# Taking out the filler matmuls in front of transposes, scores and router steps

## The chip, the cores and the metric

The kernel runs on one core of a Trainium2 chip. The metric is the device time of one execution in microseconds (us); before the change it was 1500.9 us, the median of three runs (1500.2 to 1502.37).

A core has several engines, each with its own instruction stream: TensorE (PE in the profile; its weight loads are shown apart as PEld), VectorE (DVE), ScalarE (ACT), GpSimd (POOL) and SyncE (SP), which issues the DMAs here. They meet through semaphores: an instruction adds to one, and another engine waits until it has reached a value. TensorE's clock is granted at one of two levels in this trace, 1.00 (2.4 GHz) and 0.50 (1.2 GHz).

## The reference

Two decoder layers on 256 tokens of width 1024, in float32. Each layer adds a token mixer and a channel mixer to the residual x.

```
h    = rms_norm(x, attn_norm_g[layer]);  cols = h @ w_in[layer]
o_a  = mla_mixer(cols A)            # latent attention, 4 heads, causal
o_b  = swa_sink_mixer(cols B)       # window 128, 8 query / 2 key heads, sinks
o_c  = stick_breaking_mixer(cols C) # 4 heads
x    = x + concat(rms_norm each of o_a, o_b, o_c) @ w_out[layer]
h    = rms_norm(x, ffn_norm_g[layer])
x    = x + swiglu(h, dense weights)          # layer 0, hidden width 2816
x    = x + moe_swiglu(h, router, experts)    # layer 1, top 2 of 8, width 3584
```

## The kernel before, in words

Tokens lie in two tiles of 128 (a = 0, 1), the width in eight parts of 128 (k). Weights stream from HBM in units of 2 MB into a ring of seven slots. Each unit is cut into pieces of 1024 columns. Every piece is split into a high part in fp32r (ScalarE, L867, L1016 or L1059) and the rest (VectorE, L1145, L1355 or L1491), and TensorE multiplies in three passes: high x high, high x rest, rest x high (L447 to L449). The activations are split in the same way (hT_hi, hT_lo).

The order on each engine is written out by hand, and TensorE's stream is the one that the change touches. Per layer it is: transposes of the normed input (`transposes(l, "attn_n")`), the input projection in 16 pieces with the latent up-projection among them, transposes for MLA (L500), for window attention (L511, L517) and for stick-breaking (L525), the stick-breaking scores (L538, L540), the scores of MLA and of window attention (L545, L546), the cumulative sums of stick-breaking (L565 to L569), the transposes of probabilities (L575) and the products with the values (L580 to L583), the transposes of the mixed heads (`transposes(l, "mix_n")`), the output projection, and the transposes of the second norm (`transposes(l, "ffn_n")`). Layer 0 goes on with the dense stage. Layer 1 goes on with `experts_prepare`: router logits (L682), then ranks in each expert by five small matmuls (L687 to L691). `experts` then gathers each expert's tokens by matmuls with a selection matrix (L708, L710) and runs over the eight experts.

`transposes` issues 16 transposes (L440) of xn. ScalarE and VectorE copy and split the results out of PSUM (L855, L1135), and the first product waits for the first two parts. The inputs come from a norm: ScalarE squares (L831), a chain of small steps on both engines gives the scale, and both engines write the scaled rows (ScalarE L836 or, for the mixed heads, L994; VectorE L1117 or L1331).

`stay_warm(bank, times)` (L426 to L429) issues matmuls of the identity with 512 columns of constants into a PSUM bank, and nothing reads the result. It is called in nine places in the text. Each float32 matmul of this shape leaves two records in the trace.

Of the kernel before, what the change touches and what calls it, by code (L numbers as in the profile page):

```python
# [176 lines left out]
class Counts:  # L177
# [6 lines left out]
    def at(self, key, it=None, back=0):  # L184
        if self.known is None:
            return 1 if it is None else it + 1
        name, loop, start, m = self.known[key]
        if loop is None:
            return m
        k = self.known["per", loop, name]  # L190
        if it is None:
            return start + (NE - 1) * k + m
        assert start + m - back * k > 0
        return it * k + (start + m - back * k)
# [10 lines left out]
def trunk_program(nc, known, x, cst, smalls, w_in, w_uq, w_ukv, w_out, dense_g, dense_u, dense_d, moe_g, moe_u,  # L205
# [3 lines left out]
    with ExitStack() as ctx:  # L209
        def sb(name, shape, dt=F32):  # L210
            return ctx.enter_context(nc.sbuf_tensor(name, shape, dt))
# [6 lines left out]
        consts = sb("consts", [P, N_CONST])  # L218
# [17 lines left out]
        ps = ctx.enter_context(nc.psum_tensor("ps", [P, 8, 512], F32))  # L236
# [62 lines left out]
        def C(name):  # L299
            a, w = CONST[name]  # L300
            return consts[:, a:a + w]

        def G(name, l=None):
            a, w = SMALL[name] if l is None else SMALL[name, l]
            return small[:, a:a + w]

        ident = C("ident")
# [115 lines left out]
        def _(pe):  # L423
            more = []

            def stay_warm(bank, times):  # L426

                for _ in range(times):
                    pe.matmul(ps[:, bank, :], ident, consts[:, 0:512], start=True, stop=True)  # L429

            def transposes(l, what):

                b0 = 4 if what == "ffn_n" else 0
                if what != "attn_n" or l:
                    stay_warm(0, {"mix_n": 4, "ffn_n": 4, "attn_n": 4}[what])
                for a in range(TT):
                    pe.wait_ge(act_done if a else dve_done, at((what, l, a)))
                for k in range(KD):
                    for a in range(TT):
                        ins = pe.transpose(ps[:, b0 + k // 2, (k % 2) * T + a * P:(k % 2) * T + (a + 1) * P],  # L440
                                           xn[:, a, k * P:(k + 1) * P], ident)
                    if k % 2 == 1:
                        ins.then_inc(pe_done, pe_p.step((what + "_T", l, k // 2)))
# [6 lines left out]

            def layer_mixers(l):
                transposes(l, "attn_n")

                def up_projection():
# [49 lines left out]
                for a in range(TT):  # L504
                    pe.wait_ge(*cols_in_sbuf(l, 2, a))
                pe.wait_ge(const_loaded, 16)
                stay_warm(4, 2)
                pe.wait_ge(dve_done, at(("swa_n", l)))
                for i in range(4):
                    for a in range(TT):  # L510
# [19 lines left out]
                pe.wait_ge(act_done, at(("stickT", l, 0)))  # L530
                pe.wait_ge(dve_done, at(("stickT", l, 1)))
                pe.wait_ge(act_done, at(("mlaT", l, 1)))
                stay_warm(1, 1)
                pe.wait_ge(dve_done, at(("stickT", l, 1)))
                for h in range(HC):
                    o, j = HD * (h % 2), h // 2
# [2 lines left out]
                              start=True, stop=False, skip_group_check=True)  # L539
                    ins = pe.matmul(ps[:, 4 + h, T:SEG], stick_kT[o:o + HD, j, P:T], stick_qT[o:o + HD, j, P:T],  # L540
                                    start=False, stop=False, skip_group_check=True)
# [43 lines left out]
                    ins.then_inc(pe_done, pe_p.step(key))  # L585

                pe.wait_ge(dve_done, at(("sB_read", l, 0)))
                stay_warm(0, 2)
                for h in range(HA):
                    pe.wait_ge(act_done, at(("pA", l, h)))  # L590
                    pe.wait_ge(dve_done, at(("w_read", l, h)))
# [11 lines left out]
                for h in range(HB):  # L603
                    bank = (6, 7, 0, 1, 3, 6, 7, 0)[h]
# [16 lines left out]

                pe.wait_ge(dve_done, at(("oB_read", l, 1)))
                transposes(l, "mix_n")
                for q in range(N_OUT):
                    (_, n), r = L_PIECES[l][q]
# [3 lines left out]
                    for a in range(TT):  # L629
                        for k in (2 * r, 2 * r + 1):  # L630
# [3 lines left out]
                                               k == KD - 1)  # L634
                    ins.then_inc(pe_done, pe_p.step(("piece", l, q)))
                transposes(l, "ffn_n")

            def dense(l):
# [35 lines left out]
            def experts_prepare():  # L674
                l = DEPTH - 1
                pe.wait_ge(small_loaded, 16)

                for i, k in enumerate((0, 1, 4, 5, 2, 3, 6, 7)):
                    if k % 2 == 0:
                        pe.wait_ge(act_done if k < 4 else dve_done, at(("ffn_n_done", l, k // 2)))  # L680
                    for a in range(TT):
                        ins = pe.matmul(ps[:, a, 0:NE], hT[:, k, a * P:(a + 1) * P],  # L682
                                        G("router")[:, k * NE:(k + 1) * NE], start=i == 0, stop=i == KD - 1)
                ins.then_inc(pe_done, pe_p.step("logits"))
                stay_warm(3, 3)
                pe.wait_ge(dve_done, at("selected"))
                pe.matmul(ps[:, 2, 0:NE], C("rank_tri"), sel[:, 0, :], start=True, stop=True)  # L687
                pe.matmul(ps[:, 2, NE:2 * NE], C("ones"), sel[:, 0, :], start=True, stop=False)
                pe.matmul(ps[:, 2, NE:2 * NE], C("rank_tri"), sel[:, 1, :], start=False, stop=True)
                pe.matmul(ps[:, 2, 2 * NE:3 * NE], C("ones"), sel[:, 0, :], start=True, stop=False)  # L690
                ins = pe.matmul(ps[:, 2, 2 * NE:3 * NE], C("ones"), sel[:, 1, :], start=False, stop=True)  # L691
                ins.then_inc(pe_done, pe_p.step("ranks"))

            def experts(group):
                g = group

                def gather(key, it=None):

                    pe.wait_ge(dve_done, at((g, key, "pick"), it))
                    for n in range(2):  # L700
                        if it is not None:

                            pe.wait_ge(dve_done, at((g, "hidT_lo", NCH - 2 - n), it))
                        for k in range(4):
                            for a in range(TT):

                                dims = slice((4 * n + k) * P, (4 * n + k + 1) * P)
                                pe.matmul(ps[:, 6 + n, k * P:(k + 1) * P], xn_hi[:, a, dims], pick[:, a, :],  # L708
                                          start=a == 0, stop=False, skip_group_check=True)
                                ins = pe.matmul(ps[:, 6 + n, k * P:(k + 1) * P], xn_lo[:, a, dims], pick[:, a, :],  # L710
                                                start=False, stop=a == TT - 1, skip_group_check=True)
                        ins.then_inc(pe_done, pe_p.step((g, key, "gathered", n)))
# [7 lines left out]
                                        start=True, stop=True)  # L720
                        ins.then_inc(pe_done, pe_p.step((g, "scatter" + key, q)))

                if g == 0:
                    stay_warm(6, 3)
                gather("first")
                if g == 0:
                    more.append(pe.value_load(over_i[0:1, 0:1], min_val=0, max_val=1))
# [70 lines left out]

            pe.wait_ge(ident_loaded, 16)
            layer_mixers(0)  # L800
            dense(0)
            pe.wait_ge(dve_done, at(("ffn_add", 0, 1)))
            layer_mixers(1)
            experts_prepare()
            experts(0)
            with pe.If(more[0] > 0):
                experts(1)
# [794 lines left out]
```

## Time and profile before

| | |
|---|---|
| median of three runs | 1500.9 us (1500.2 to 1502.37) |
| span of the profiled execution | 1498.5 us |
| TensorE busy | 1458.0 us (97%), 7282 matmul records |
| weight loads | 1209.2 us (81%) |
| VectorE busy | 1210.2 us (81%) |
| ScalarE busy | 1046.6 us (70%) |
| mean granted clock of TensorE | 0.992 |
| HBM | 415.23 MB read, 278 GB/s |

The span runs from the first to the last instruction of the program in one profiled execution; the timed runs are other executions. Busy shares are averages over the whole span. The layers and the work ahead of the experts make up its first 484 us, and the eight experts the rest.

In the rows further down, a row in order of time gives the start and the length in us, engine, line, operation, what it writes and reads, the shape and the number of records merged into it; in brackets the idle time of the engine ahead of it and who ended that. The length of a merged row reaches from its first start to its last end, and records can overlap.

### The profile page before, as it was taken

Reading aid. Unit: us, or ns where it says so; the run is one execution under the profiler, and the core shown is the slowest. Engines: PE = TensorE matmul, PEld = TensorE weight load, DVE = VectorE, ACT = ScalarE, POOL = GpSimd, SP = SyncE. Lnnn points to the kernel's source line nnn. Section 1 sums busy time; section 2 is a strip of 40 time slices with the busy share of each in tenths; the row PEclk is TensorE's granted clock in tenths of the full one; section 3 lists DMA queues with packets and bytes.
Section 4 is the critical chain, followed back from the end, with each engine's and each line's share of the span. In section 5 each row is a group of like instructions: output and inputs, shape, how many; then the busy total and the mean of one; then the engine's idle time right before and its main releaser. Section 6 shows DMA issues by size and latency. Waiting matters only on the chain.

```text
span 1498.5 us, 21039 instructions
## 1 busy us (share of the span) xinstructions
PE 1458.0 (97%) x7282; PEld 1209.2 (81%) x7282; DVE 1210.2 (81%) x1501; ACT 1046.6 (70%) x1452; POOL 0.2 (0%) x4
## 2 busy tenths in 40 slices
PE   7999999999998999999999999999999999999997
PEld 6777999978775788888888878888888887888885
DVE  5666555546765899899899999989989999998995
ACT  5675444435764788788788778878878877887884
POOL 0000000000000000000000000000000000000000
PEclk9999999999998999999999999999999999999999
DMA  9904444454111899899989989989999998998960
GB/s 365 347 1 169 169 169 141 164 219 169 57 58 56 301 372 380 305 373 365 349 330 376 368 311 374 376 306 370 367 347 333 372 370 313 372 372 314 374 225 30
DMA packets 175806, 416.90 MB, mean 278 GB/s; under 512 B 3344, under 2 KB 8080, under 8 KB 175632
## 3 DMA queue, kind: packets, MB, share of 16 engines
q1 hardware_dynamic: 175760, 416.29, 76.1%
q8 instruction: 28, 0.46, 0.1%
q14 instruction: 18, 0.15, 0.0%
HBM read 415.23 MB, written 1.05 MB: 278 GB/s over the span
## 4 chain that ended last, share of the span: by engine, by line
PE 92%; DVE 4%; ACT 3%; issue 1%; DMA 0%; DVEq 0%; SPq 0%; ACTq 0%
PE ps L447 27%; PE ps L448 27%; PE ps L449 27%; PE ps L719 2%; PE ps L742 2%; PE ps L710 1%; PE ps L708 1%; PE ps L429 1%; DVE scratch L1247 1%; PE ps L575 1%; ACT scratch L908 1%; PE ps L580 0%; PE ps L583 0%; PE ps L581 0%; ACT xn L831 0%
## 5 line engine op out<-in xcount | busy, mean ns | idle before, releaser
L1059 ACT ACTIVATE e_hi<-ring 128x1024 fp32r<-128x1024 f32 x672 | 712.2, 1061 | 200.4 <-PE ps L449 200.4
L1491 DVE TENSOR_TENSOR e_lo<-ring,e_hi 128x1024 fp32r<-128x1024 f32 x672 | 793.2, 1219 | 63.9 <-ACT e_hi L1059 47.4
L447 PE MATMUL ps<-e_hi,xgT_hi 128*128 128x512 f32 x896 | 357.2, 399 | 3.5 <-DVE e_lo L1491 3.5
L449 PE MATMUL ps<-e_hi,xgT_lo 128*128 128x512 f32 x896 | 349.9, 391 | 0.0
L448 PE MATMUL ps<-e_lo,xgT_hi 128*128 128x512 f32 x896 | 349.8, 390 | 0.0
L447 PEld LDWEIGHTS ps<-e_hi,xgT_hi 128*128 128x128 f32 x896 | 168.9, 188 | 38.9 <-DVE e_lo L1491 3.7
L448 PEld LDWEIGHTS ps<-e_lo,xgT_hi 128*128 128x128 f32 x896 | 168.9, 188 | 35.4 <-issue 1.9
L449 PEld LDWEIGHTS ps<-e_hi,xgT_lo 128*128 128x128 f32 x896 | 168.6, 188 | 35.6
L1355 DVE TENSOR_TENSOR d_lo<-ring,d_hi 128x1024 fp32r<-128x1024 f32 x82 | 100.2, 1224 | 95.0 <-ACT d_hi L1016 94.7
L447 PE MATMUL ps<-e_hi,hidT_hi 128*128 128x512 f32 x448 | 175.7, 392 | 0.0
L449 PE MATMUL ps<-e_hi,hidT_lo 128*128 128x512 f32 x448 | 174.5, 390 | 0.0
L448 PE MATMUL ps<-e_lo,hidT_hi 128*128 128x512 f32 x448 | 174.4, 389 | 0.0
L1016 ACT ACTIVATE d_hi<-ring 128x1024 fp32r<-128x1024 f32 x82 | 87.0, 1061 | 112.1 <-PE ps L449 112.1
L447 PE MATMUL ps<-hT_hi,d_hi 128*128 128x256 f32 x352 | 99.7, 283 | 1.0 <-DVE hT_lo L1135 1.0
L449 PE MATMUL ps<-hT_hi,d_lo 128*128 128x256 f32 x352 | 99.6, 283 | 0.0
L448 PE MATMUL ps<-hT_lo,d_hi 128*128 128x256 f32 x352 | 99.6, 283 | 0.0
L449 PEld LDWEIGHTS ps<-e_hi,hidT_lo 128*128 128x128 f32 x448 | 84.1, 188 | 17.8
L448 PEld LDWEIGHTS ps<-e_lo,hidT_hi 128*128 128x128 f32 x448 | 84.2, 188 | 17.0
L447 PEld LDWEIGHTS ps<-e_hi,hidT_hi 128*128 128x128 f32 x448 | 84.1, 188 | 16.9
L447 PEld LDWEIGHTS ps<-hT_hi,d_hi 128*128 128x128 f32 x352 | 67.6, 192 | 1.4 <-DVE hT_lo L1135 1.2
L448 PEld LDWEIGHTS ps<-hT_lo,d_hi 128*128 128x128 f32 x352 | 67.6, 192 | 0.2
L449 PEld LDWEIGHTS ps<-hT_hi,d_lo 128*128 128x128 f32 x352 | 67.6, 192 | 0.0
(233 smaller groups left out, 1648.9 us busy)
## 6 DMA issues: line engine op xcount, KB each, us to landing
ring<-moe_g SPq DMA_DIRECT2D x56, 2048.0 KB, 9.0
ring<-moe_u SPq DMA_DIRECT2D x56, 2048.0 KB, 9.4
ring<-moe_d SPq DMA_DIRECT2D x56, 2048.0 KB, 8.5
ring<-w_in SPq DMA_DIRECT2D x6, 2048.0 KB, 10.8
ring<-dense_g SPq DMA_DIRECT2D x5, 2048.0 KB, 8.0
ring<-dense_u SPq DMA_DIRECT2D x5, 2048.0 KB, 8.1
ring<-dense_d SPq DMA_DIRECT2D x5, 2048.0 KB, 8.8
ring<-w_out SPq DMA_DIRECT2D x4, 2048.0 KB, 14.3
```

The costliest lines, as they stand in the source:

```text
L429: pe.matmul(ps[:, bank, :], ident, consts[:, 0:512], start=True, stop=True)
L447: pe.matmul(out, hi_l, hi_r, start=start, stop=False, skip_group_check=True)
L448: pe.matmul(out, hi_l, lo_r, start=False, stop=False, skip_group_check=True)
L449: return pe.matmul(out, lo_l, hi_r, start=False, stop=stop, skip_group_check=True)
L575: ins = pe.transpose(ps[:, bank, j * P:(j + 1) * P], S[:, slot, j * P:(j + 1) * P], ident)
L708: pe.matmul(ps[:, 6 + n, k * P:(k + 1) * P], xn_hi[:, a, dims], pick[:, a, :], start=a == 0, stop=False, skip_group_check=True)
L719: ins = pe.matmul(ps[:, bank, :], pick_gT[:, a, :], ysb[:, n * CH:(n + 1) * CH], start=True, stop=True)
L742: ins = pe.transpose(ps[:, bank, j * P:(j + 1) * P], hid[:, c % 2, j * P:(j + 1) * P], ident)
L1016: nc.scalar.activation(d_hi[:, q % SPLIT, :], slot_of(no)[:, r * PIECE:(r + 1) * PIECE], ACT.Copy).then_inc(act_done, act_p.step(("lead", ...
L1059: nc.scalar.activation(e_hi[:, q % SPLIT, :], slot_of(no)[:, r * PIECE:(r + 1) * PIECE], ACT.Copy).then_inc(act_done, act_p.step((g, "lead ...
L1355: nc.vector.tensor_tensor(d_lo[:, q % SPLIT, :], slot_of(UNIT_NO[kind, l, c])[:, r * PIECE:(r + 1) * PIECE], d_hi[:, q % SPLIT, :].bitcast ...
L1491: nc.vector.tensor_tensor(e_lo[:, q % SPLIT, :], slot_of(no)[:, r * PIECE:(r + 1) * PIECE], e_hi[:, q % SPLIT, :].bitcast(F32), ALU.subtra ...
```

## The change

All nine calls of `stay_warm` and the helper itself are taken out. The calls stood: at the head of `transposes` (four matmuls each for mix_n and ffn_n of both layers, and for attn_n of layer 1; none for attn_n of layer 0); in front of the window-attention transposes (two); in front of the stick-breaking scores (one); in front of the transposes of MLA probabilities (two); behind the router logits (three); and in front of the first gather (three). That makes 36 matmuls in one execution. Every wait stays where it was, and no other instruction changes.

```
-            def stay_warm(bank, times):
-                for _ in range(times):
-                    pe.matmul(ps[:, bank, :], ident, consts[:, 0:512], start=True, stop=True)
...
                 b0 = 4 if what == "ffn_n" else 0
-                if what != "attn_n" or l:
-                    stay_warm(0, {"mix_n": 4, "ffn_n": 4, "attn_n": 4}[what])
                 for a in range(TT):
                     pe.wait_ge(act_done if a else dve_done, at((what, l, a)))
...
                 pe.wait_ge(const_loaded, 16)
-                stay_warm(4, 2)
                 pe.wait_ge(dve_done, at(("swa_n", l)))
...
                 pe.wait_ge(act_done, at(("mlaT", l, 1)))
-                stay_warm(1, 1)
                 pe.wait_ge(dve_done, at(("stickT", l, 1)))
...
                 pe.wait_ge(dve_done, at(("sB_read", l, 0)))
-                stay_warm(0, 2)
                 for h in range(HA):
                     pe.wait_ge(act_done, at(("pA", l, h)))
...
                 ins.then_inc(pe_done, pe_p.step("logits"))
-                stay_warm(3, 3)
                 pe.wait_ge(dve_done, at("selected"))
...
-                if g == 0:
-                    stay_warm(6, 3)
                 gather("first")
```

## Rows read from the trace of the kernel before

**Rows 1.** The page's chain of work that ended last, by engine.

```profile
PE 92%; DVE 4%; ACT 3%; issue 1%; DMA 0%; DVEq 0%; SPq 0%; ACTq 0%
```

**Rows 2.** Instructions of line 429: duration ns min/median/max, first and last start, shape.

```profile
L429 PE MATMUL ps<-consts x72: 590/592/1222, 65.0 to 475.4; 128*128 128x512 f32 x72
```

**Rows 3.** TensorE in order of time, window-attention transposes and stick-breaking scores, layer 0.

```profile
65.03 1.88 PE L429 MATMUL ps<-consts 128*128 128x512 f32 x4
66.75 1.04 PE L511 MATMUL ps<-consts,scratch 128*128 128x128 f32 x8
...
69.71 1.10 PE L429 MATMUL ps<-consts 128*128 128x512 f32 x2 [0.83 <-ACT stick_qT L932]
70.73 0.71 PE L538 MATMUL ps<-stick_qT,stick_kT 64*128 64x256 f32 x4
```

**Rows 4.** VectorE in order of time, the same stretch.

```profile
65.81 0.28 DVE L1235 TENSOR_TENSOR cols<-cols,stat 128x128 f32<-128x128 f32 x1
...
68.92 0.69 DVE L1242 COPY stick_kT<-ps 128x512 f32<-128x512 f32 x1
```

**Rows 5.** TensorE in order of time, transposes of the mixed heads, layer 0.

```profile
102.75 5.34 PE L429 MATMUL ps<-consts 128*128 128x512 f32 x8 [0.85 <-DVE xn L1300]
107.93 1.91 PE L440 MATMUL ps<-consts,xn 128*128 128x128 f32 x16
110.37 0.50 PE L447 MATMUL ps<-d_hi,hT_hi 128*128 128x512 f32 x1 [0.53 <-DVE hT_lo L1135]
```

**Rows 6.** ScalarE and VectorE in order of time, the same stretch.

```profile
105.70 1.52 ACT L994 ACTIVATE xn<-xn,stat 128x256 f32<-128x256 f32 x3 [0.70 <-DVE stat L1109]
...
108.27 1.23 DVE L1355 TENSOR_TENSOR d_lo<-ring,d_hi 128x1024 fp32r<-128x1024 f32 x1 [1.56 <-ACT d_hi L1016]
```

**Rows 7.** TensorE in order of time, transposes of the second norm, layer 0.

```profile
132.27 3.59 PE L429 MATMUL ps<-consts 128*128 128x512 f32 x8
138.25 1.94 PE L440 MATMUL ps<-consts,xn 128*128 128x128 f32 x16 [2.38 <-ACT xn L836]
141.20 0.36 PE L447 MATMUL ps<-hT_hi,d_hi 128*128 128x256 f32 x1 [1.01 <-DVE hT_lo L1135]
```

**Rows 8.** ScalarE and TensorE in order of time, start of layer 1.

```profile
333.21 1.15 ACT L836 ACTIVATE xn<-xres,stat 128x1024 f32<-128x1024 f32 x1 [0.70 <-DVE stat L1109]
...
335.90 1.91 PE L440 MATMUL ps<-consts,xn 128*128 128x128 f32 x16
338.34 0.46 PE L447 MATMUL ps<-in_hi,in_hT_hi 128*128 128x416 f32 x1 [0.53 <-DVE in_hT_lo L1135]
...
338.64 0.35 PE L448 MATMUL ps<-in_lo,in_hT_hi 128*128 128x416 f32 x1
```

**Rows 9.** TensorE in order of time, transposes of MLA probabilities, layer 0.

```profile
81.59 1.88 PE L429 MATMUL ps<-consts 128*128 128x512 f32 x4
83.79 1.91 PE L575 MATMUL ps<-consts,scratch 128*128 128x128 f32 x12 [0.32 <-DVE stick L1289]
```

**Rows 10.** TensorE in order of time, the kernel's start, and the router.

```profile
10.57 3.57 PE L440 MATMUL ps<-consts,xn 128*128 128x128 f32 x16 [10.57 <-ACT xn L836]
...
14.38 0.35 PE L448 MATMUL ps<-in_lo,in_hT_hi 128*128 128x416 f32 x1
...
462.51 1.94 PE L440 MATMUL ps<-consts,xn 128*128 128x128 f32 x16 [2.38 <-ACT xn L836]
464.29 3.64 PE L682 MATMUL ps<-small,hT 128*128 128x8 f32 x32
```

**Rows 11.** Stretches: length, TensorE busy (records), granted clock, DMA share, GB/s.

```profile
467.91:471.31 3.40, 3.40 (x6) 0.50 0.00 0
477.07:480.90 3.83, 3.79 (x32) 1.00 0.01 2
...
484.38:488.38 4.00, 4.00 (x9) 0.50 0.00 0
```

**Rows 12.** VectorE in order of time, ahead of the read of the ranks.

```profile
472.77 2.36 DVE L1435 TENSOR_TENSOR xn_lo<-xn,xn_hi 128x1024 fp32r<-128x1024 f32 x2
```

More of the change, by code:

```diff
@@ L424, in _ @@
             more = []
-            def stay_warm(bank, times):
-                for _ in range(times):
-                    pe.matmul(ps[:, bank, :], ident, consts[:, 0:512], start=True, stop=True)
             def transposes(l, what):
                 b0 = 4 if what == "ffn_n" else 0
-                if what != "attn_n" or l:
-                    stay_warm(0, {"mix_n": 4, "ffn_n": 4, "attn_n": 4}[what])
                 for a in range(TT):
@@ L506, in layer_mixers @@
                 pe.wait_ge(const_loaded, 16)
-                stay_warm(4, 2)
                 pe.wait_ge(dve_done, at(("swa_n", l)))
@@ L532, in layer_mixers @@
                 pe.wait_ge(act_done, at(("mlaT", l, 1)))
-                stay_warm(1, 1)
                 pe.wait_ge(dve_done, at(("stickT", l, 1)))
@@ L587, in layer_mixers @@
                 pe.wait_ge(dve_done, at(("sB_read", l, 0)))
-                stay_warm(0, 2)
                 for h in range(HA):
@@ L684, in experts_prepare @@
                 ins.then_inc(pe_done, pe_p.step("logits"))
-                stay_warm(3, 3)
                 pe.wait_ge(dve_done, at("selected"))
@@ L721, in scatter @@
                         ins.then_inc(pe_done, pe_p.step((g, "scatter" + key, q)))
-                if g == 0:
-                    stay_warm(6, 3)
                 gather("first")
```

## The prediction

> **What bounds the kernel now.** I read the chain of work that ended last first. TensorE holds 92% of it [rows 1], and nearly all of that is the matrix products of the two dense stages and of the eight experts, which the change does not touch. So only those stretches count in which a removed matmul stands on the chain, or in which its absence changes the clock that the next work gets. The second view is the list of one line's instructions: the helper's line 429 has 72 records on TensorE, 592 ns median [rows 2]. A call leaves two records, so 36 filler matmuls run. Four of them took 3.59 us in one place, 0.9 us each, and 5.34 us, partly at the low clock, in another [rows 5, 7]. The third view is the order of time around each call, to see what the next real instruction was waiting for. The fourth is the granted clock by stretch. It shows two levels, 1.00 (2.4 GHz) and 0.50 (1.2 GHz).
>
> **Where a filler itself is in the way (the gains).**
>
> (a) Before the window-attention transposes. The filler runs at 65.03 and the transposes (L511) start at 66.75 [rows 3], but their input is there when VectorE's L1235 ends at 65.81 + 0.28 = 66.09 [rows 4]. From the end of L1242 at 68.92 + 0.69 = 69.61 to TensorE's next start at 69.71 [rows 3, 4] a hand-over takes 0.10 us. So 66.75 - 66.19 = 0.56 us goes. The next in line, VectorE's L1239, is free by then.
>
> (b) Before the stick-breaking scores. All waits are met when the filler starts at 69.71, and the scores start at 70.73 [rows 3]. The whole 1.02 us is in series, and the chain goes on through these scores.
>
> Both come once in each layer, with the same durations in the second: 2 x (0.56 + 1.02) = 3.2 us.
>
> (c) Before the second layer's first transposes. The last input is ScalarE's L836, 333.21 + 1.15 = 334.36, but the transposes start at 335.90, when eight filler records are through [rows 8]. They can start near 334.5, 1.4 us sooner. At the low clock the first four of them take about 0.85 us instead of 0.45, so 1.0 us reaches the ScalarE and VectorE copies behind them and the first product at 338.34.
>
> Gains together: 3.2 + 1.0 = 4.2 us. They are nearly certain, since each is a stretch in which the real work had been ready. Ends: 3.6 and 4.6.
>
> **Where a filler is hidden.** In front of the mixer-output transposes the fillers end late (the transposes start at 107.93 [rows 5], ScalarE's L994 had been done at 105.70 + 1.52 = 107.22 [rows 6]). But the first product, at 110.37, waits for VectorE: L1355 from 108.27 to 109.50 and then two parts of the split [rows 6]. Starting TensorE 0.6 us sooner brings nothing there. In front of both ffn_n transposes the engine was idle for another 2.38 us after the filler [rows 7]. In front of the attention probabilities' transposes the filler begins at 81.59 and L575 waits until 83.79 for VectorE [rows 9]. The five rank matmuls, each of 8 columns, are read by VectorE only after L1435, at 472.77 + 2.36 = 475.13 [rows 12], which leaves room for them at either clock. In front of the gather, TensorE waits for VectorE's pick until 477.07. Taking all these away gives nothing directly; what it does is leave the engine without work.
>
> **What the clock does (the costs).** The clock was at 0.50 from 467.91 to 471.31, after 3.6 us of router matmuls with 8 columns each [rows 10, 11]; it fell again after the gather and stayed low through the first 4.00 us of the expert products, until 488.38 [rows 11]. At the kernel's start, where TensorE had done nothing, 16 transposes took 3.57 us against 1.91 to 1.94 elsewhere, and a 416-column product right behind them, at 14.38, took 0.35 us, the same as one at 338.64 deep in layer 1 [rows 5, 7, 8, 10]. So a burst after a long idle stretch runs at half rate for about 3.5 us, and 4.0 us is the longest that a row shows. That is the price list.
>
> (d) Four places: mix_n in both layers, ffn_n in the first, attn_n in the second. Without filler TensorE has nothing for 5.4 to 6.0 us ahead of its transposes (102.75 - 0.85 = 101.9 to 107.3, and 132.27 to 138.25 [rows 5, 6, 7]; the start of layer 1 waits for the same chain of a norm), so I take it that they begin at 1.2 GHz. They then take 3.57 us, but in pairs, and each pair is followed by ScalarE and VectorE work of about the same length. The product streams start 2.4 (107.93 to 110.37) to 2.95 us (138.25 to 141.20) after the transposes do [rows 5, 7], or 3.1 with the earlier start at mix_n. So 0.4 to 0.6 us of the stream is still at half rate, 0.2 to 0.3 us each: 0.9 us for the four. Ends: 0 (the clock back sooner) and 2.0 (4.0 us low).
>
> (e) ffn_n of the second layer and the router: TensorE is the chain here, 16 transposes in 1.94 us and then 32 router records in 3.64 [rows 10]. The transposes at half rate add 1.65 us. The router's records are as dense as the transposes' and should double too if the clock is low; by rows, thin router work began at 464.29 and lost the clock only at its end, so I add only 0.15: 1.8 us. Ends: 0.3 and 3.5.
>
> (f) The gather: 32 matmuls in 3.83 us at clock 1.00 [rows 11], with a filler ahead of it. Now the engine has only 8-column work from 464.29 [rows 10] and, while VectorE works from 475.13 on [rows 12], none before 477.07. It starts low. With 3.5 us at half rate the price is 1.7; if its 128-column matmuls don't bring the clock back, 3.8. No row shows a gather at a low clock; what it is nearest to is a clock that fell right after it, so I take 2.5, above the middle of 1.0 and 3.8.
>
> (g) The 2.2 us between 81.59 and 83.79 [rows 9] become empty, and the chain gives all of 83.79 to 101.9 to TensorE. A gap of 2.38 us kept its clock at 138.2 [rows 7]; a gap of 0.85 us behind the 64-column products with the values lost it, as the eight filler records of 5.34 us tell [rows 5]. If the clock falls here, about 3.4 us run at half: 1.7 us a layer. I take one layer of the two: 1.7. Ends: 0 and 3.4.
>
> Expert products 484.38 to 488.38: low before and after, no change.
>
> **Sum.** 0.9 + 1.8 + 2.5 + 1.7 - 4.2 = +2.7 us. On the profiled execution's own 1498.5 us span that is 1501.2; the timed runs' median lies 2.4 us higher, at 1500.9, so 1503.6.
>
> One page speaks against this sum. The Trainium skill, "TensorE: Matmul & The Clock Gate", Part 4: PE-mode transpose, says that transposes don't count as activity for the clock. The trace disagrees as far as it goes: the start's 16 transposes were the only work before products that ran at the full rate [rows 10].
>
> **Rivals.**
>
> *The clock mostly holds.* (g) costs nothing and the gather only 1.7: 1503.6 - 1.7 - 0.8 = 1501.1. For it: 2.38 us of idle time were survived [rows 7]. Against: there a dense product stream stood ahead. Chance 0.27.
>
> *Thin work stays slow* (the one that ends slower). Place: the 18 us from 83.79, and the gather. Price: (g) in both layers, +1.7, and the gather at half rate throughout, +1.3: 1506.6. It decides when the gap at 81.59 loses the clock in both layers, and it is past the bound from the moment that the second of these falls happens. For it: the clock did fall behind 64-column products. Chance 0.17.
>
> *Transposes don't bring the clock back.* Then the product stream behind each of the four places of (d) itself runs 3.4 us at half, 1.7 us each in place of 0.23, and the router is slow whole, +3.6: 1503.6 + 5.9 + 3.6 = 1513. This is what the page's rule named above would make of it; the start of the trace speaks against it. Chance 0.05.
>
> *The waits cover the low clock.* The clock comes back early (ends of d, e and g) and the gather pays 1.0: 1500.9 + 0 + 0.3 + 1.0 + 0 - 4.2 = 1498.0. Against: (e) and (f) are on the chain with nothing beside them. Chance 0.09. That the fillers are not really gone is excluded: the diff leaves no call.
>
> **How the numbers follow.** 0.2% is 3.0 us here, about what the measurement can tell from no change, so slower begins at 1503.9 and faster ends at 1497.9. The forecast's case has 0.42, from 1502.3 to 1505, of which 0.19 lies beyond 1503.9. Slower: 0.19 + 0.17 + 0.05 = 0.41. Faster: 0.09 at most. Same: 0.50. The range leaves out the 1513 case, most of the 1498 case and the outer parts of the others: 1499.8 to 1507.8. Both kernels vary from execution to execution with where the clock falls, which the three runs' 2.2 us of spread allow.
>
> **What would show it.** Right: first window-attention transposes about 0.5 us after TensorE's last transposes of MLA, no record between L932 and L538, 16 transposes of 3 to 3.6 us at mix_n and ffn_n with a granted clock of 0.50, transposes and router together near 7.3 us, gather of 5.5 to 7.5 us, first product of mix_n at the same distance from ScalarE's L994. Wrong: 16 transposes of 1.9 us in these places, a gather of 3.8 us (then it is faster), or a clock of 0.50 through the attention values or deep in a product stream (then it is slower than the range's middle).

## The result, and the profile after

The change makes the kernel slower: 1514.03 us median of five runs (1503.79 to 1517.23) against 1500.9 us (1500.2 to 1505.69), a ratio of 1.0074 with a 95% interval of 1.0041 to 1.0108. A repetition on another occasion gave 1.0131 (1.0079 to 1.0182). The prediction was 1503.6, with a range of 1499.8 to 1507.8. It was wrong.

The single runs say more than the median. Here are all nine of the changed kernel, with the mean granted clock of each:

```
us     1503.79  1513.45 1513.47 1513.69 1514.03 1517.10 1517.23  1525.87 1527.17
clock    0.979    0.974   0.974   0.974   0.974   0.972   0.972    0.967   0.965
```

They stand in three groups some 10 us apart, and the time rises as the mean clock falls. The first trace of the changed kernel is of the one run in the lowest group. It is 3.4 us longer than the traced run of before (spans 1501.9 and 1498.5), near the forecast sum of 2.7, and that this one run falls so close to 1503.6 is the luck of the draw. So that trace alone can't tell why most runs are slow; a second one, below, can.

TensorE in order of time in the first trace, window-attention transposes and stick-breaking scores; these answer to [rows 3]:

```profile
66.53 1.06 PE L503 MATMUL ps<-consts,scratch 128*128 128x128 f32 x8 [1.04 <-DVE cols L1222]
...
69.56 0.71 PE L529 MATMUL ps<-stick_qT,stick_kT 64*128 64x256 f32 x4 [0.87 <-DVE stick_kT L1229]
```

And VectorE in the same stretch, answering to [rows 4]:

```profile
66.10 0.28 DVE L1222 TENSOR_TENSOR cols<-cols,stat 128x128 f32<-128x128 f32 x1
...
68.73 0.69 DVE L1229 COPY stick_kT<-ps 128x512 f32<-128x512 f32 x1
```

Both now start 0.14 to 0.15 us after their input ends (66.38 and 69.42). The fillers that stood in between are really gone, and so is their time. (The calls taken out stand in six places of the text, as the edit shows, and not in nine; the count of 36 matmuls is right.)

TensorE in order of time at the transposes of the mixed heads (L433, then the products L440), of the second norm in layer 0, and at the start of layer 1. These answer to [rows 5, 7, 8]:

```profile
106.17 3.32 PE L433 MATMUL ps<-consts,xn 128*128 128x128 f32 x16 [5.47 <-ACT xn L981]
109.24 0.48 PE L440 MATMUL ps<-d_hi,hT_hi 128*128 128x512 f32 x1
...
137.10 3.65 PE L433 MATMUL ps<-consts,xn 128*128 128x128 f32 x16 [5.82 <-ACT xn L823]
140.40 0.56 PE L440 MATMUL ps<-hT_hi,d_hi 128*128 128x256 f32 x1
140.75 0.41 PE L441 MATMUL ps<-hT_lo,d_hi 128*128 128x256 f32 x1
...
334.91 3.30 PE L433 MATMUL ps<-consts,xn 128*128 128x128 f32 x16 [6.41 <-ACT xn L823]
337.96 0.43 PE L440 MATMUL ps<-in_hi,in_hT_hi 128*128 128x416 f32 x1
...
429.73 3.65 PE L433 MATMUL ps<-consts,xn 128*128 128x128 f32 x16 [5.47 <-ACT xn L981]
```

The last row is the same place as the first, in layer 1. All the transposes run at half rate, as forecast. At 140.75 a 256-column product still does, 0.41 us a record where the full clock gives 0.28.

Stretches of the same trace: length, TensorE busy (records), granted clock, DMA share, GB/s. They answer to [rows 11]:

```profile
82.60:102.18 19.58, 18.10 (x148) 1.00 0.01 2
102.20:109.01 6.81, 2.85 (x14) 0.50 0.00 1
136.33:143.14 6.81, 6.04 (x29) 0.50 0.41 138
330.89:337.70 6.81, 2.79 (x13) 0.50 0.01 1
406.50:426.45 19.95, 17.77 (x147) 1.00 0.01 2
426.47:433.27 6.80, 3.54 (x17) 0.50 0.00 0
...
467.43:491.30 23.87, 13.51 (x54) 0.50 0.00 0
476.80:484.40 7.60, 7.08 (x32) 0.50 0.00 1
```

The first and fifth rows are the probability transposes, scores and values of the two layers, at the full clock in this execution. From the router's end to the first expert products the clock is low for 23.87 us, and the gather takes 7.08 us of TensorE instead of 3.79.

And the router, answering to [rows 10]:

```profile
461.01 3.39 PE L433 MATMUL ps<-consts,xn 128*128 128x128 f32 x16 [5.82 <-ACT xn L823]
464.24 3.94 PE L672 MATMUL ps<-small,hT 128*128 128x8 f32 x32
```

### The profile page after: what moved, and what is told of

Same layout as the page of the kernel before. It is cut to its first block, busy times and chain, and to the rows that moved or that the text cites. A ratio compares the mean times of both kernels' runs of the same rounds, so it can differ in the third digit from the quotient of the medians.

```text
span 1501.9 us, 20899 instructions
## 1 busy us (share of the span) xinstructions
PE 1432.2 (95%) x7210; PEld 1207.3 (80%) x7210; DVE 1210.4 (81%) x1501; ACT 1046.9 (70%) x1452; POOL 0.2 (0%) x4
## 4 chain that ended last, share of the span: by engine, by line
PE 92%; DVE 4%; ACT 2%; issue 1%; DMA 1%; SPq 0%; DVEq 0%; ACTq 0%
PE ps L440 27%; PE ps L441 27%; PE ps L442 27%; PE ps L708 2%; PE ps L729 2%; PE ps L699 1%; PE ps L697 1%; PE ps L433 1%; DVE scratch L1234 1%; PE ps L566 1%; DMA ring<-w_in 1%; ACT scratch L895 1%; PE ps L571 0%; PE ps L574 0%; PE ps L572 0%
## 5 line engine op out<-in xcount | busy, mean ns | idle before, releaser
L440 PE MATMUL ps<-e_hi,xgT_hi 128*128 128x512 f32 x896 | 357.4, 399 | 3.5 <-DVE e_lo L1478 3.5
L440 PEld LDWEIGHTS ps<-e_hi,xgT_hi 128*128 128x128 f32 x896 | 168.8, 188 | 38.8 <-DVE e_lo L1478 3.7
L440 PE MATMUL ps<-e_hi,hidT_hi 128*128 128x512 f32 x448 | 175.8, 392 | 0.0
L440 PE MATMUL ps<-hT_hi,d_hi 128*128 128x256 f32 x352 | 100.4, 285 | 0.0
L440 PEld LDWEIGHTS ps<-e_hi,hidT_hi 128*128 128x128 f32 x448 | 84.2, 188 | 16.9
L440 PEld LDWEIGHTS ps<-hT_hi,d_hi 128*128 128x128 f32 x352 | 68.3, 194 | 0.2
```

The lines of the kernel that those rows point to most:

```text
L440: pe.matmul(out, hi_l, hi_r, start=start, stop=False, skip_group_check=True)
```

## The experiments

Means below are over all runs of a kernel, set against the mean of the runs of before in the same batch. The ratio with its interval is a separate estimate from the same runs; it can differ from the quotient of the means by some 0.1% (most in the next experiment: 1.0131, where the means give 1.0114).

**The changed kernel again.**

> The changed kernel unchanged, for a second trace. In its first profiled execution (1501.9 us span, mean granted clock 0.979) the clock kept its full level through the attention values of both layers; the other four runs had spans of 1511.8 to 1515.1 us at a mean clock of 0.974 and 0.972. Theory T1 (the empty gap ahead of the probability transposes loses the clock and the thin products with the values don't get it back): if this execution is a long one, a stretch between about 82 and 102 us, or its twin 324 us later, stands at 0.50 for 10 us or more. Theory T2 (the extra time lies at the router, the gather and the first expert products): those two stretches stand at 1.00 and more of the low clock than before lies between 460 and 500 us. Median expected 1514, with single runs from 1503 to 1518.

Measured: 1519.67 us median of four (1513.45 to 1527.17), ratio 1.0131 (1.0079 to 1.0182). The traced execution had a span of 1511.4 us, of the middle group. Stretches of this trace, the same columns:

```profile
81.00:101.95 20.95, 18.11 (x148) 1.00 0.01 2
405.75:426.21 20.46, 20.46 (x88) 0.50 0.00 1
...
477.43:501.31 23.88, 13.51 (x53) 0.50 0.00 0
```

This is what the first trace could not show. Layer 0 went through its probability transposes, scores and values at 1.00. Layer 1, with the same instructions, went at 0.50 for 20.46 us in which TensorE was busy all the time. At half the rate that is 10.2 us more, the distance between the groups. T1 stands. T2, as the cause of the long runs, does not: the low stretch from the router's end to the first expert products is 23.88 us here and was 23.87 in the short run's trace, and transposes and router together took 7.26 us (from 470.19 to 477.45) against 7.17.

**Only the fillers in the probability gap put back.**

```
+                stay_warm(0, 2)            # ahead of the probability transposes
                 for h in range(HA):
```

> The changed kernel with only the two filler matmuls ahead of the probability transposes put back, in each layer. T1: the long executions vanish, all runs between 1502 and 1506 us, mean clock 0.979 or above. T2: as the changed kernel, most runs at 1513 to 1517.

Measured: 1505.87 median of ten (1503.44 to 1509.65), ratio 1.0024 (1.0010 to 1.0037). No run at 1513 or above. Four runs lie above the expected 1506, at mean clocks of 0.978 and 0.979. These four matmuls (two in each layer) of the 36 are worth 10 us: the mean is 1506.2 against 1516.2 for the nine runs of the changed kernel. Against the mean of before, 1502.8, the other 32 taken out cost 3.4 us (1.5 to 5.6 by the interval), where the prediction's sum without its term (g) has 1.0.

**Only these taken out.**

```
                 pe.wait_ge(dve_done, at(("sB_read", l, 0)))
-                stay_warm(0, 2)
```

> The kernel before with only these two filler matmuls per layer taken out. T1: most runs 8 to 13 us longer than before, so 1509 to 1514, at a mean clock about 0.985; a few at 1501. T2: 1500 to 1502.5, as before.

Measured: 1510.49 median of ten, ratio 1.0052 (1.0018 to 1.0085); mean 1511.0 against 1502.8. The runs again fall into groups:

```
1500.88 1501.16 | 1509.58 1510.07 1510.41 1510.57 1510.61 1511.78 | 1521.54 1523.03
```

Two runs stand where before stands, six some 10 us above, two some 20 us above. With 10.2 us for a layer that reads as none, one and both; a trace shows it for the middle group alone. Stretches of the traced run (1510.07):

```profile
84.00:104.50 20.50, 18.71 (x150) 1.00 0.01 2
408.90:429.36 20.46, 20.46 (x88) 0.50 0.01 2
```

One trace holds both outcomes behind the same idle gap. In order of time, the gap in layer 0, where the clock stayed up:

```profile
82.52 0.39 PE L569 MATMUL ps<-stick,consts 128*128 128x128 f32 x2
84.94 1.91 PE L575 MATMUL ps<-consts,scratch 128*128 128x128 f32 x12 [2.04 <-DVE stick L1288]
```

and in layer 1, where it fell at 408.9, with what followed:

```profile
405.80 0.39 PE L569 MATMUL ps<-stick,consts 128*128 128x128 f32 x2
408.23 2.45 PE L575 MATMUL ps<-consts,scratch 128*128 128x128 f32 x12 [2.04 <-DVE stick L1288]
410.61 0.79 PE L545 MATMUL ps<-swa_kT,swa_qT 64*128 64x128 f32 x2
...
416.51 0.64 PE L581 MATMUL ps<-mla_v,hT 128*128 128x64 f32 x2
...
426.32 2.77 PE L575 MATMUL ps<-consts,scratch 128*128 128x128 f32 x12
...
429.74 0.39 PE L580 MATMUL ps<-cols,hT 128*128 128x64 f32 x2
```

The gap is 2.04 us in both, so its length alone doesn't decide. The clock then stayed low through 12 transposes, the eight 64-row score matmuls of four heads and 24 products of 64 columns (0.64 us for two records against 0.39), and came back only behind the next 12 transposes.

That the empty gap is what lets the clock fall rests on all traces together. Four traces have the gap empty (two of the changed kernel, this one and the next), and in three of the eight passages the clock fell at it, each time in layer 1. In the nine other traces, of before and of the further experiments, the filler stands in the gap, and in none of the 18 passages did a low stretch begin between it and the end of the products with the values.

**A late filler.** Does a fallen clock stay low for a fixed 20 us, or until denser work comes?

```
-                stay_warm(0, 2)            # the probability gap
...
                 for h in range(HA):
                     pe.wait_ge(*probs_in_sbuf(l, "A", h))
+                    if h == 0:
+                        stay_warm(4, 2)
                     values(probsT[:, h, :], ...)
```

> As the kernel with the two probability fillers taken out, but with two 512-column matmuls per layer put behind the first wait of the products with the values, where TensorE is on the chain. In two traces the clock fell at the empty gap and stayed at 0.50 for 20.5 us both times. Theory T1a (the 64-column products can't raise it, dense work can): the low stretch ends within some 7 us behind the late filler, long runs shrink from 1510 and 1521 to 1504 to 1512; runs without a fall pay 1.7 us per layer and stand at 1504. T1b (a fallen clock stays low for a fixed 20 us whatever is run): the low stretch is again 20.5 us, the runs stay at 1510 and more, and the filler adds 3 us to them. In either case the fall itself comes as often as without the filler, since that comes too late for it.

Measured: 1510.53 median of ten (1508.25 to 1517.44), ratio 1.0063 (1.0046 to 1.0080). Its stretch, and TensorE in order of time at the late filler in layer 0, at the full clock, and in layer 1:

```profile
411.06:421.28 10.22, 10.22 (x27) 0.50 0.01 2
```

```profile
89.13 1.98 PE L429 MATMUL ps<-consts 128*128 128x512 f32 x4
...
416.33 1.06 PE L546 MATMUL ps<-swa_kT,swa_qT 64*128 64x256 f32 x2
417.32 3.78 PE L429 MATMUL ps<-consts 128*128 128x512 f32 x4
420.89 0.53 PE L580 MATMUL ps<-mla_v,hT 128*128 128x64 f32 x2
421.48 0.39 PE L583 MATMUL ps<-mla_v,hT 128*128 128x64 f32 x2
```

The low stretch was 10.22 us, not 20.46, and it ended 4 us behind the start of the filler, as the first 64-column products began. So the duration isn't fixed: T1b falls, T1a stands. The longest runs shrank from 1523 to 1517, not to 1512. The traced run, 1508.75, is one of the shortest, and it had one fall, in layer 1: 5.1 us for the half rate and some 1.8 us for each layer's filler are 8.7 us on top of before's short runs at 1500.5. By this estimate the six runs from 1508.3 to 1511.0 had one fall, the four from 1513.9 on two, and none was without. In the kernels with the empty gap 3 runs of 19 were without; whether their absence here is more than chance is open. As a repair it is useless, since the filler is on the chain here.

**The three late places.**

```
-                if what != "attn_n" or l:
-                    stay_warm(0, {"mix_n": 4, "ffn_n": 4, "attn_n": 4}[what])
+                stay_warm(0, {"mix_n": (4, 4), "ffn_n": (4, 0), "attn_n": (0, 4)}[what][l])
...
-                stay_warm(3, 3)            # behind the router logits
...
-                if g == 0:
-                    stay_warm(6, 3)        # ahead of the first gather
```

> The kernel before without three of its filler places: ahead of the second norm's transposes in layer 1, behind the router logits and ahead of the first gather. This measures terms (e) and (f) by themselves. Prediction: 1.8 + 2.5 = 4.3 us longer. The changed kernel's trace says more for (f): its 32 gather matmuls took 7.1 us in place of 3.8, so 1.8 + 3.3 = 5.1 us. The values of both layers should keep their full clock in the trace. Rival: the time is with the values alone (the first comparison put 10 us there), and this one is under 2 us.

Measured: 1510.09 median of ten (1505.47 to 1512.15), ratio 1.0044 (1.0029 to 1.0058); mean 1509.4 against 1502.3, so 7.1 us. In its trace the clock was low through everything from the second norm to the first expert products, and the router took double:

```profile
461.15:498.67 37.52, 25.06 (x103) 0.50 0.02 3
```

```profile
463.24 3.65 PE L439 MATMUL ps<-consts,xn 128*128 128x128 f32 x16 [5.82 <-ACT xn L832]
466.68 6.83 PE L681 MATMUL ps<-small,hT 128*128 128x8 f32 x32
```

Transposes and router took 10.3 us here, 7.2 in the changed kernel's first trace, 5.4 in before. The mean is neither the prediction's 4.3 nor the rival's "under 2".

**These places apart.**

> The kernel before with only the three filler matmuls ahead of the first gather taken out. By the two traces in which the gather ran wholly at the low clock (7.1 us in place of 3.8) it is 3.3 us longer, 1505. Prediction's term (f): 2.5. Rival: with the filler behind the router logits in place the clock is up when the ranks are done, the gather starts at the full clock, and it costs under 1 us.

Without the gather's three matmuls alone: 1505.19 median, ratio 1.0019 (1.0005 to 1.0032), mean 1505.8 against 1503.1, so 2.7 us. Term (f) was 2.5. The rival falls by the trace, where the gather ran low although a filler stood behind the router logits; the interval of the time alone (0.8 to 4.8 us) would still hold its "under 1 us".

```profile
477.48:491.11 13.63, 10.11 (x40) 0.50 0.00 1
```

> The kernel before without the fillers ahead of the second norm's transposes in layer 1 and behind the router logits. Transposes and router together took 5.4 us in the trace of before, 7.2 in that of the changed kernel and 10.4 in that of the kernel without all three late places. So between 1.8 and 5.0 us longer, by which of the two an execution draws; 3.4 in the mean, 1505.5. Prediction's term (e): 1.8.

Without the second norm's in layer 1 and the router's: 1507.11 median, ratio 1.0025 (1.0014 to 1.0036), mean 1506.8 against 1503.1, so 3.7 us. Term (e) was 1.8. The two add up to 6.4, near the 7.1 of both at once. TensorE in order of time in the trace (run of 1505.14):

```profile
462.56 3.65 PE L439 MATMUL ps<-consts,xn 128*128 128x128 f32 x16 [5.82 <-ACT xn L834]
466.00 3.99 PE L681 MATMUL ps<-small,hT 128*128 128x8 f32 x32
...
475.95 5.02 PE L429 MATMUL ps<-consts 128*128 128x512 f32 x6
480.40 0.62 PE L706 MATMUL ps<-pick,xn_hi 128*128 128x128 f32 x1
```

Transposes and router took 7.4 us, 2.0 more than in before. The rest arose behind them: the fillers that still stood ahead of the gather ran mostly at the low clock, 5.02 us in place of 2.82, and the gather began at 480.40, which is 3.3 us later than in before. The changed kernel has no such fillers, so this run overstates what term (e) cost there.

**The four other starts of a stage.**

```
-                if what != "attn_n" or l:
-                    stay_warm(0, {"mix_n": 4, "ffn_n": 4, "attn_n": 4}[what])
+                stay_warm(0, {"mix_n": (0, 0), "ffn_n": (0, 4), "attn_n": (0, 0)}[what][l])
```

> The kernel before without the fillers ahead of the mixed heads' transposes (both layers), of the second norm's in layer 0 and of layer 1's first ones. This measures (d) less (c). Prediction: 0.9 - 1.0, so no change within 1 us. Rival, the rule that transposes don't bring the clock back: product streams of the four places at half for 3.4 us each, 6 us longer.

Measured: 1503.86 median of ten (1502.39 to 1507.36), ratio 1.0007 (0.9996 to 1.0019), mean 1504.3 against 1502.3. That is 1.9 us by the means and 1.1 by the ratio, where no change within 1 us was expected. The interval, -0.6 to 2.9 us, holds no change; the 6 us of the rival are excluded. The trace shows where the products of layer 0's output projection started at half rate:

```profile
107.96 3.65 PE L439 MATMUL ps<-consts,xn 128*128 128x128 f32 x16 [5.47 <-ACT xn L993]
111.26 0.78 PE L446 MATMUL ps<-d_hi,hT_hi 128*128 128x512 f32 x1
...
113.52 0.39 PE L448 MATMUL ps<-d_hi,hT_lo 128*128 128x512 f32 x1
```

The clock was back 5.5 us after the first transpose here, not 3.5, and 2.2 us of the product stream ran low.

**The fillers in the way.**

```
-                stay_warm(4, 2)            # ahead of the window-attention transposes
-                stay_warm(1, 1)            # ahead of the stick-breaking scores
```

> The kernel before without the fillers ahead of the window-attention transposes and of the stick-breaking scores, three matmuls per layer. By gains (a) and (b) of the prediction 3.2 us less: 1497.7. A rival: with them gone the stretch from 66 to 70 us is thin enough to lose the clock, and some runs are 3 us or more longer instead, 1502 to 1505.

Measured: 1499.46 median of ten (1497.14 to 1505.63), ratio 0.9985 (0.9969 to 1.0000), mean 1499.9 against 1502.8: 2.9 us less for a forecast of 3.2. The interval reaches up to no change. In its trace the stretch from 64 to 72 us and its twin in layer 1 keep the full clock. One run at 1505.63 is like the longest of before, so this doesn't speak for the rival.

**The fillers moved.**

```
-                if what != "attn_n" or l:
-                    stay_warm(0, {"mix_n": 4, "ffn_n": 4, "attn_n": 4}[what])
+                if what == "ffn_n":
+                    stay_warm(0, 6)
...
-                stay_warm(4, 2)
...
-                stay_warm(1, 1)
...
+                stay_warm(0, 6)
                 pe.wait_ge(dve_done, at(("oB_read", l, 1)))
                 transposes(l, "mix_n")
...
                 gather("first")
+                if g == 0:
+                    stay_warm(3, 2)
...
+            stay_warm(0, 7)
             pe.wait_ge(dve_done, at(("ffn_add", 0, 1)))
             layer_mixers(1)
```

> A version meant to beat both. The two fillers in the way are out (3 us in the last comparison). Those of the mixed heads and of layer 1's start stand ahead of their wait instead of behind it, six and seven matmuls, so that the engine is never idle for them; the second norm's are six; two new ones stand behind the first gather, where the clock fell in every trace and the first expert products ran 4.0 us at half. Expected: 1502.2 - 3.2 - 1.4 (layer 1 starts when its input is there) - 1.5 (first expert products) = 1496 us, with mean clock 0.997 and a smaller spread. Rival: fillers that themselves run at the low clock are late for the work behind them, as at 330.67 to 336.06 in the trace of before, and eat the gain: 1499.

Measured: 1496.21 us median of five (1494.39 to 1496.72), ratio 0.9952 (0.9934 to 0.9970). TensorE in order of time at the start of layer 1:

```profile
333.19 1.94 PE L440 MATMUL ps<-consts,xn 128*128 128x128 f32 x16 [0.41 <-ACT xn L838]
335.73 0.45 PE L447 MATMUL ps<-in_hi,in_hT_hi 128*128 128x416 f32 x1 [0.61 <-DVE in_hT_lo L1137]
```

The transposes wait for ScalarE and not for a filler, and they run at the full rate. Up to the gather the clock never fell:

```profile
14.60:475.35 460.75, 445.81 (x2665) 1.00 0.44 159
475.37:482.17 6.80, 6.79 (x19) 0.50 0.00 0
```

All five runs lie within 2.3 us, where the runs of before spread over 5.7. The fillers behind the gather ran low here (3.72 us for two matmuls), and the clock was back 0.7 us into the expert products, where before it took 4.0. From the first expert product to the end this trace has 1012.6 us and before's 1014.1, the 1.5 that were expected. What the moved fillers of the mixed heads and of layer 1's start are worth was not measured apart.

> The version with the moved fillers, with four matmuls instead of three ahead of the first gather, so that the idle stretch between them and the gather shrinks from 1.4 us to 0.5. In the trace of that version the clock fell once, at 475.4 during the gather (32 matmuls in 4.7 us instead of 3.8). If that idle stretch is what lost it: 1 us less, 1495. If it is the gather's own 128-column matmuls: unchanged at 1496.

With one more matmul ahead of the gather: 1496.28 median of six (1494.51 to 1497.96), ratio 0.9951 (0.9932 to 0.9969). In its trace the clock stayed up through the gather, but fell once ahead of it, from 469.4 to 472.8, during the filler behind the router:

```profile
469.41:472.80 3.39, 3.39 (x6) 0.50 0.00 0
```

The 1 us expected for the idle stretch did not come. The question of the run stays open: the fillers, partly at the low clock, left no idle time at all ahead of this gather, and it kept its clock, but the gather of before kept it too, with 1.1 us of idle time ahead.

## Why the prediction was wrong, point by point

**What bounds the kernel.** Right. From the first expert product to the end the traces have 1013.7 to 1015.4 us (before 1014.1, the changed kernel 1014.0 and 1014.2), but for the two versions with a filler behind the gather; nearly every difference arose ahead of it and was carried through whole.

**Gains (a) and (b), 3.2 us.** Right: 2.9 measured alone. **(c), 1.0 us.** About right: from the last product of layer 0 to the first of layer 1 were 9.5 us in the changed kernel's first trace (337.96 less 328.5, where the idle time of 6.41 began) and 10.2 in before (338.34 less 328.1), a gain of 0.8.

**Hidden fillers cost nothing directly.** Right at the full clock. A filler that itself runs at the low clock can come to stand in the way, as the run without the second norm's and the router's showed ahead of the gather.

**(d), 0.9 us.** Perhaps too small; the times can't tell. With (c) in it, the four places cost 1.9 us in the mean and 1.1 by the ratio, where the sum had -0.1, and the interval holds all three. The term took the kernel's start (3.5 us) for the usual delay. In the first trace of the changed kernel the clock came back 2.8, 6.0, 2.8 and 3.5 us after the first transpose (106.17 to 109.01, 137.10 to 143.14, 334.91 to 337.70, 429.73 to 433.27), and 5.5 us after it in the run without these fillers. That the start ran at half rate was itself read from durations; the column of the granted clock has 1.00 there:

```profile
10.52:13.93 3.41, 3.36 (x16) 1.00 1.03 396
```

**(e), 1.8 us.** Right in the changed kernel's two traces: transposes and router took 7.2 and 7.3 us against 5.4. But it has a dear outcome too. In the trace without the three late places the router ran at the low clock throughout, 6.83 us, and the two took 10.3, 4.9 more than in before, beyond the upper end of 3.5. How often that happens is not known.

**(f), 2.5 us.** Right: 2.7 alone. In both traces of the changed kernel the gather took 7.1 us, 3.3 more than in before and short of the upper end of 3.8.

**(g), 1.7 us.** This is the step that failed. The place was named, and "one layer of the two" is what most runs showed: six of nine, with one at none and two at both. The price was wrong by a factor of six: a fall cost 10.2 us and not 1.7. It assumed that a fall lasts about 3.4 us, taken from falls after which dense work stood waiting: fillers, or products of 512 columns. Here 64-row scores and 64-column products followed, and the stretch was 20.46 us in two traces. The prediction's own rival ("thin work stays slow") had this mechanism, and it too priced it at 1.7 a layer. It named the 18 us of TensorE's work from 83.79 on as its place. Half rate over all of it would have been 18 us more in a layer; the falls in the traces ended after 20.46 us, which hold 10.2 us of that work, and cost 10.2.

**The sum by measured parts.** 8.1 (probability gap) + 7.1 (three late places) + 1.9 (four starts) - 2.9 (in the way) = 14.2 us by means. The whole change measured 13.4 (1516.2 against 1502.8). The agreement is partly luck: the nine runs of the changed kernel scatter by 7 us each, so their mean is uncertain by some 5 us. And all but the probability gap measured 3.4 when taken out together, where the parts give 6.1. Either way the gap holds 8 to 10 us of the whole, for the 1.7 that (g) had.

**Transposes that don't count.** The rival of 1513 us came near the number, but the time did not come from its mechanism. In the first trace TensorE was idle until 106.17, ran only transposes, and the clock was back at 109.01, ahead of the first product at 109.24; the same holds at the start of layer 1 (334.91, 337.70 and 337.96). The Trainium skill, "TensorE: Matmul & The Clock Gate", Part 4: PE-mode transpose, says that transposes don't count as activity for the clock. These rows disagree, and so does the run without the four starts' fillers, where the rival had 6 us and the interval ends at 2.9. But transposes don't always suffice: without the three late places 16 of them, from 463.24 on, left the clock at 0.50, and the router behind them ran low whole, which was the other half of that rival.

**The time and its chances.** One trace of before showed no fall of the clock in the attention stages, and the range was built on small prices. Since the same instructions lose the clock in one execution and keep it in the next, the range needed the dear outcome of each layer at its full price: 0, 10 and 20 us on top.

What stays open: what makes one execution lose the clock in a gap and the next keep it, with the same instructions. Open too is why each traced fall in the gap was layer 1's, and which property of the 64-row and 64-column work keeps the clock down. And the kernel before has runs at 1505 to 1507.6 as well (mean clock 0.990 to 0.993, mostly 0.990, against 0.991 to 0.996 in the others), of which no trace was taken.

## What to carry to other kernels

A filler matmul is worth what the work behind it would lose at half clock, which is half of the low stretch that would follow. Judge the length of that stretch by the work that stands there, not by a low stretch seen elsewhere: it was 20.46 us where 64-row and 64-column work followed. Take fillers out where the real work is ready, since there they are plain time (2.9 us here). Putting them ahead of the wait that they bridge, sized to end just before it is met, was part of the version that came out 6 us ahead of before, though its parts were not measured one by one. Time a change of this sort in ten runs, look at the mean clock of each, and don't read a cause from one trace when the runs stand in groups.

## What the hardware showed that was not expected

A busy TensorE can stay at 0.50: 20.46 us without any idle time, in two executions, through transposes, 64-row scores and 64-column products. With two 512-column float32 matmuls put into it, in one execution, the low stretch ended about 4 us later. The same gap of 2.04 us kept the clock in layer 0 and lost it in layer 1 of one execution. The router's 32 matmul records of 8 columns took 3.64 us at the full clock and 6.83 at the low one, 1.9 times as long, so this work follows the clock nearly as fully as wide matmuls do.
